# Scatter DMAs of the expert gates in groups of four behind waits for ScalarE, and the low parts of 24 weight units made by VectorE instead of GpSimd

## The chip, the cores and the metric

One core of one Trainium2 chip runs the whole program. The time is device microseconds of one execution; the times below are those of several executions and their median, and a profile is one further execution under the profiler.

## What is computed

Two transformer blocks over 512 tokens of width 1024, in fp32. The change lies in the expert layer (PEER) of the first block:

```python
q = (ht @ wq).reshape(T, PEER_HEADS, 2, PEER_HALF)
sc = jnp.einsum('thpd,hpnd->thpn', q, subkeys)
v1, i1 = lax.top_k(sc[:, :, 0], PEER_TOPK)          # 8 heads, 16 best of 128 keys, twice
v2, i2 = lax.top_k(sc[:, :, 1], PEER_TOPK)
cand = (v1[..., :, None] + v2[..., None, :]).reshape(T, PEER_HEADS, PEER_TOPK * PEER_TOPK)
best, pos = lax.top_k(cand, PEER_TOPK)
experts = e1 * PEER_KEYS + e2                        # 128 experts of 16384 for each token
gates = jax.nn.softmax(best, axis=-1)
act = jax.nn.gelu(jnp.einsum('tkd,td->tk', u_tab[experts], x))
out = jnp.einsum('tk,tkd->td', gates * act, v_tab[experts])
```

Before it stand sliding-window attention and a pooling mixer, after it the second block: differential attention, a short convolution and two gated feed-forward layers.

## The kernel before

**Units.** All weights are 486 units of 128 x 1024 fp32 (512 KB). A unit is loaded by the queue of SP into a ring of eight buffers (`RING`), ScalarE rounds it to its high part (`split_hi`, L1062), and the low part, raw minus high, is made in the place of the raw data by GpSimd (`low_part`, L509, four quarters of 256 columns) or by VectorE (`unit_low`, L1765, in one instruction). A product with it is three matmuls (`mm3`, L593 to L595): high by high, low by high, high by low. TensorE starts a unit when its low part is there (`unit_in`) and signals `unit_used` at its end; ScalarE makes the high part of unit u + 5 after that of unit u (`AHEAD`), and SP loads unit u + 8.

**The stage of the expert scores** multiplies all 16384 rows of `u_tab` (key units 0 to 127, 24 matmuls of 512 columns each) with the 512 tokens; after each unit ScalarE applies the gelu (L1264) and every four units stores 1024 KB to `act_dram`. Beside it VectorE, in one fixed order of instructions, selects the experts of the token tiles 1, 2, 3, 0 (`select`), and for tiles 1 to 3 sums the gates of equal experts (`join_gates`: seven steps of growing size, 128x512 to 128x2048, on `same` and `gate_sums`) and gives them free for scattering (`gates_made`). Low parts of key units from 28 on (`LOW_FROM`) are placed between these steps by `lows(n)`. From unit 56 on VectorE makes one low part per unit and two products of the modulation sums of the second block (`ada_part`, L1781 and L1783; two instructions a tile for the first 16 tiles, one for the other 80), whose 96 tiles of 512 KB SP loads from unit 51 on, two a unit; TensorE adds a short sum after every fourth unit (`ada_sum`). This is the ada stage below, units 56 to 103.

**The scatters.** GpSimd writes the gates of tiles 1 to 3 into a dense table `gate_dram` (128 units x 128 rows x 384 tokens) with 384 indirect DMAs of 128 elements (`scatter`, L547), 16 to a token tile and head, in the order of `SCATTERS`; a tile's next head waits until the one before has landed. Before the change GpSimd also makes the low parts of 24 key units (`BESIDE`: 30, 34, 38, 42, 47, ... 127), a quarter after each four scatters; before the first quarter it waits for the unit's high part. So the scatters are held to the pace of the units. After unit 124 (`LOADS_AT`) ScalarE waits for all scatters and loads the first gates and activations.

**The stage of the expert values** multiplies gates and activations (`gp`, 384 tokens) with `v_tab`, 128 value units; the 128 tokens of tile 0 are done by gathering rows instead (L533, L541, L1945).

The lines that count in what follows: L509 GpSimd's quarter, L547 the scatter, L593 to L595 the matmuls of a unit, L1062 a high part, L1264 the gelu, L1274 and L1280 the loads of gates and activations, L1765 VectorE's low part, L1781 and L1783 the ada products. Unit numbers are those of key units unless value units are named.

Of the kernel before, what the change touches and what calls it, by code (L numbers as in the profile page):

```python
# [16 lines left out]
F32 = mybir.dt.float32  # L17
# [4 lines left out]
ALU = mybir.AluOpType  # L22
AX_X = mybir.AxisListType.X

P = 128
D = 1024
# [16 lines left out]
TOPK = 16  # L43
# [10 lines left out]
U_PEER = U_WQ + 2 * PEER_HEADS  # L54
# [3 lines left out]
U_DIFF = U_PEER + 2 * P  # L58
# [8 lines left out]
RING = 8  # L67
# [8 lines left out]
LOW_FROM = 28  # L76
ORDER = (1, 2, 3, 0)
EXP_AT = (5, 17, 29, 45)
SCATTERS = [(1, 0), (2, 0), (1, 1), (2, 1)] + [s for h in range(6) for s in ((3, h), (1, h + 2), (2, h + 2))] \
    + [(3, 6), (3, 7)]  # L80
BESIDE = [30 + 17 * n // 4 for n in range(len(SCATTERS))]
ZEROS = 8
LOADS_AT = P - 4
BUNCH = 4
SPAN = 8
ROWS = 4
# [1 line left out]
LAG = AHEAD - 1  # L88
# [30 lines left out]
def build_program(nc, w_units, x_in, ctx_in, params, consts, consts2, trig, pool_w, subkeys, ada_w, out,  # L119
                  rel_dram, gate_dram, act_dram, x_dram):  # L120
    KB = 1024
    with ExitStack() as ctx:
# [16 lines left out]
        hi = at("unit_hi", 0, [P, RING, D], F32R)  # L139
        lo = at("unit_lo", 32 * KB, [P, RING, D], F32R)  # L140
        raw = at("unit_raw", 32 * KB, [P, RING, D])
# [166 lines left out]
        hi_ready, lo_ready, unit_used = sem("hi_ready"), sem("lo_ready"), sem("unit_used")  # L308
        value_lo_ready = sem("value_lo_ready")
# [194 lines left out]

        @block.gpsimd
        def _(pool):
            def quarter(u, part):
                cols = slice(part * (D // 4), (part + 1) * (D // 4))
                return nc.gpsimd.tensor_tensor(lo[:, u % RING, cols], raw[:, u % RING, cols],  # L509
                                               hi[:, u % RING, cols].bitcast(F32), ALU.subtract)  # L510

            def low_part(u, per=0, i=None):

                pool.wait_ge(hi_ready, u + 1 if i is None else i * per + (u + 1))
                for part in range(4):
                    last = quarter(u, part)
                last.then_inc(lo_ready, 1)

            def low_range(a, b):
                while a < b and a % RING:  # L520
                    low_part(a)
                    a += 1
                n = max(0, (b - a) // RING)
                if n:
                    with pool.Fori(0, n) as i:
                        for k in range(RING):
                            low_part(a + k, RING, i)
                for u in range(a + n * RING, b):
                    low_part(u)

            def pick(k):

                pool.indirect_dma_start(picked[:, k:k + 1], None, act_dram.rearrange("u j (t o) -> (u j t) o", o=1),  # L533
                                        bass.IndirectOffsetOnAxis(act_at[:, k:k + 1], 0))\
                    .then_inc(picks_in[k // PICKS], 16)

            def fetch(k):

                if k >= ROWS:
                    pool.wait_ge(row_added, k - ROWS + 1)  # L540
                pool.indirect_dma_start(vrows[:, k % ROWS, :], None, w_units.rearrange("u p n -> (u p) n"),  # L541
                                        bass.IndirectOffsetOnAxis(row_at[:, k:k + 1], 0))\
                    .then_inc(rows_in[k % ROWS], 16)

            def scatter(t, k):

                pool.indirect_dma_start(gate_dram.rearrange("i j (t o) -> (i j t) o", o=1),  # L547
                                        bass.IndirectOffsetOnAxis(gidx[:, t - 1, k:k + 1], 0),
                                        gsum[:, t - 1, k:k + 1], None).then_inc(scattered[t - 1], 16)

            nc.gpsimd.memset(zero[:, :], 0.0).then_inc(zero_made, 1)
            low_range(0, U_PEER + LOW_FROM)
            pool.wait_ge(zeroed, 16 * ZEROS)
            for n, (t, h) in enumerate(SCATTERS):
                if h == 0:
                    pool.wait_ge(gates_made, t)
                else:
                    pool.wait_ge(scattered[t - 1], 16 * TOPK * h)
                for k in range(TOPK):
                    scatter(t, TOPK * h + k)  # L560
                    if k % 4 == 3:
                        if k == 3:
                            pool.wait_ge(hi_ready, U_PEER + BESIDE[n] + 1)
                        last = quarter(U_PEER + BESIDE[n], k // 4)
                last.then_inc(lo_ready, 1)
            pool.wait_ge(mine_at, 2)
            pool.wait_ge(unit_used, U_VALUES)
            for s in a_stored:
                pool.wait_ge(s, 16 * (P // BUNCH // 2))
            for k in range(PICKS):  # L570
                pick(k)
            for k in range(ROWS):
                fetch(k)
            for k in range(ROWS, G):
                ahead = PICKS + 2 * (k - ROWS) if k < ROWS + PICKS else 2 * PICKS - ROWS + k
                for n in range(ahead, ahead + (2 if k < ROWS + PICKS else 1)):
                    if n < G:
                        pick(n)
                fetch(k)
            low_range(U_DIFF + LAG, N_UNITS)  # L580
# [3 lines left out]
        def _(pe):  # L584
# [11 lines left out]

            def unit_in(u, per=0, i=None):
                made, n = lo_ready, u + 1
                before = sum(U_PEER + b < u for b in BESIDE)
                if u - U_PEER in BESIDE:  # L600
                    n = U_PEER + LOW_FROM + before + 1
                elif U_PEER + LOW_FROM <= u < U_DIFF + LAG:
                    made, n = value_lo_ready, u + 1 - (U_PEER + LOW_FROM) - before
                elif u >= U_DIFF + LAG:
                    n -= U_DIFF + LAG - (U_PEER + LOW_FROM) - before
                pe.wait_ge(made, n if i is None else i * per + n)

            def project(u, dst, ah, al, per=0, i=None, ready=None):
# [95 lines left out]
            for n in range(10):  # L704
                u = U_WIN + n
# [4 lines left out]
                else:  # L710
                    band_scores(0)
                    unit_in(u)
                    for t in range(TT):
                        tok = slice(t * P, (t + 1) * P)
                        for c in range(DC):
                            wh, wl = unit_chunk(u, c)
                            last = mm3(ps[:, n % 4, tok], hn_hi[:, c, tok], hn_lo[:, c, tok], wh, wl,
                                       c == 0, c == DC - 1)
# [11 lines left out]
            for t in range(TT):  # L730
# [5 lines left out]
                for s in range(2 * HEADS):  # L736
                    last = nc.tensor.transpose(PTp[:, s, :], E[t][:, s // 2, (s % 2) * P:(s % 2 + 1) * P], ident)
# [776 lines left out]
        def _(dve):  # L1514
# [247 lines left out]
            def unit_low(u):  # L1762

                dve.wait_ge(hi_ready, u + 1)
                V.tensor_tensor(lo[:, u % RING], raw[:, u % RING], hi[:, u % RING].bitcast(F32),  # L1765
                                ALU.subtract).then_inc(value_lo_ready, 1)
# [33 lines left out]
            def lows(n):  # L1800

                for u in range(key_lows[0], min(key_lows[0] + n, P + LAG)):
                    if u not in BESIDE:
                        unit_low(U_PEER + u)
                key_lows[0] += n

            def select(t, between):
# [80 lines left out]
            select(1, 0)  # L1888
            join_gates(1, (0,) * 7)
            select(2, 0)  # L1890
            join_gates(2, (0, 0, 0, 0, 0, 0, 1))
            select(3, 2)
            join_gates(3, (1, 1, 2, 1, 1, 2, 1))
            select(0, 2)
# [272 lines left out]
            for j in range(DC):  # L2167
                b = j % 2
# [176 lines left out]
```

## Time and profile before

| | |
|---|---|
| runs | 3044.7, 3061.32, 3061.61 us, median 3061.32 |
| profiled execution | 3072.2 us, of which the span of the trace is 3070.4 |
| TensorE busy | 2875.8 us, 94% |
| VectorE, ScalarE, GpSimd busy | 1762.4 us (57%), 983.9 us (32%), 1704.7 us (56%) |
| mean granted clock of TensorE | 0.968 |

Busy times of engines overlap, and those of TensorE's instructions are modelled, so a busy engine is not one at its peak. A granted clock of 1.00 is 2.4 GHz, one of 0.50 is 1.2 GHz. Key units 28 to 127 lie between 442 and 1116 us of the span and the value units from 1120 on.

### The profile page before, as it was taken

What the parts mean: (1) busy time and instruction counts of PE and PEld (TensorE: products, weight loads), DVE (VectorE), ACT (ScalarE), POOL (GpSimd) and SP (SyncE); (2) the same over time, 40 slices, a digit from 0 to 9 for tenths busy, and PEclk for the clock granted to TensorE, in tenths of its full rate; (3) what the DMA queues carried; (4) which work ended last, traced back from release to release, by engine and by line L of the source; (5) the groups of instructions that cost most, each with busy time, mean ns of one, the idle gap of its engine ahead of it and who ended that gap; (6) DMA issues with size and microseconds to landing.
All of it is one profiled execution on the core that took longest, in us unless ns stands there. A gap on an engine that the chain in (4) does not pass through costs nothing.

```text
span 3070.4 us, 39204 instructions
## 1 busy us (share of the span) xinstructions
PE 2875.8 (94%) x14484; PEld 2443.1 (80%) x14484; DVE 1762.4 (57%) x2726; ACT 983.9 (32%) x1472; POOL 1704.7 (56%) x1757
## 2 busy tenths in 40 slices
PE   8799988888989988999999989999999989999999
PEld 6698877677777778999999858558888868898887
DVE  6568997665553136778887773674333353343333
ACT  4432322222222333333333433783322222232211
POOL 5144877788888755688753123002554545555553
PEclk9899999999999999999999999999999999999999
DMA  6932443378875467999997211101323323233332
GB/s 202 342 97 83 153 129 98 122 250 284 289 267 186 124 209 283 325 338 347 355 350 276 90 55 50 38 1 59 97 90 102 96 76 96 72 108 103 97 95 75
DMA packets 191662, 499.40 MB, mean 163 GB/s; under 512 B 29608, under 2 KB 80936, under 8 KB 190888
## 3 DMA queue, kind: packets, MB, share of 16 engines
q1 hardware_dynamic: 104528, 338.95, 33.4%
q10 hardware_dynamic: 52184, 91.23, 8.4%
q0 software_dynamic: 34816, 67.41, 6.3%
q8 instruction: 86, 1.41, 0.2%
q14 instruction: 48, 0.39, 0.0%
HBM read 432.82 MB, written 64.68 MB: 162 GB/s over the span
## 4 chain that ended last, share of the span: by engine, by line
PE 57%; POOL 21%; DVE 11%; issue 6%; ACT 3%; DMA 2%; another core or an unknown queue 0%; SPq 0%; ACTq 0%; DVEq 0%
PE ps L593 17%; PE ps L595 17%; PE ps L594 17%; POOL gate_dram L547 13%; POOL value_rows L541 3%; POOL picked L533 3%; POOL unit_lo L509 3%; PE ps L917 2%; DVE nb L2000 1%; PE ps L937 1%; DMA unit_raw<-w_units 1%; DVE same L1858 1%; DVE same L1856 1%; DVE gate_sums L1860 1%; PE ps L928 1%
## 5 line engine op out<-in xcount | busy, mean ns | idle before, releaser
L509 POOL TENSOR_TENSOR unit_lo<-unit_raw,unit_hi 128x256 fp32r<-128x256 f32 x1112 | 876.5, 820 | 1049.3 <-ACT unit_hi L1062 1046.5
L593 PE MATMUL ps<-hn_hi,unit_hi 128*128 128x512 f32 (+1 forms) x2344 | 922.8, 394 | 107.3 <-POOL unit_lo L509 74.1
L594 PE MATMUL ps<-hn_lo,unit_hi 128*128 128x512 f32 (+1 forms) x2344 | 904.6, 386 | 0.0
L595 PE MATMUL ps<-hn_hi,unit_lo 128*128 128x512 f32 (+1 forms) x2344 | 903.9, 386 | 0.0
L1062 ACT ACTIVATE unit_hi<-unit_raw 128x1024 fp32r<-128x1024 f32 x486 | 505.7, 1055 | 487.2 <-DMA unit_raw<-w_units 372.8
L593 PEld LDWEIGHTS ps<-hn_hi,unit_hi 128*128 128x128 f32 x2344 | 449.2, 192 | 218.6 <-issue 103.0
L594 PEld LDWEIGHTS ps<-hn_lo,unit_hi 128*128 128x128 f32 x2344 | 449.5, 192 | 88.9 <-issue 4.9
L547 POOL DMA_INDIRECT gate_dram<-gate_sums,gate_at x384 | 460.6, 1199 | 104.1 <-issue 103.4
L595 PEld LDWEIGHTS ps<-hn_hi,unit_lo 128*128 128x128 f32 x2344 | 448.3, 191 | 87.8
L1765 DVE TENSOR_TENSOR unit_lo<-unit_raw,unit_hi 128x1024 fp32r<-128x1024 f32 x208 | 259.8, 1250 | 185.9 <-ACT unit_hi L1062 150.1
L593 PE MATMUL ps<-gp_hi,unit_hi 128*128 128x384 f32 x1024 | 349.2, 341 | 18.2 <-DVE gp_lo L1927 14.2
L595 PE MATMUL ps<-gp_hi,unit_lo 128*128 128x384 f32 x1024 | 346.8, 339 | 3.9 <-issue 3.9
L594 PE MATMUL ps<-gp_lo,unit_hi 128*128 128x384 f32 x1024 | 346.9, 339 | 3.1 <-issue 3.0
L1264 ACT ACTIVATE stage<-ps 128x512 f32<-128x512 f32 x128 | 76.5, 598 | 610.1 <-PE ps L595 570.8
L541 POOL DMA_INDIRECT value_rows<-w_units,row_at x128 | 191.1, 1493 | 123.5 <-DVE own_values L1945 79.8
L2128 DVE TENSOR_TENSOR pf<-gel,ps 128x512 f32<-128x512 f32 x44 | 30.3, 688 | 380.8 <-PE ps L595 380.8
L593 PEld LDWEIGHTS ps<-gp_hi,unit_hi 128*128 128x128 f32 x1024 | 195.6, 191 | 24.0 <-DVE gp_lo L1927 13.8
L533 POOL DMA_INDIRECT picked<-act_dram,act_at x128 | 176.0, 1375 | 62.4 <-issue 38.7
L595 PEld LDWEIGHTS ps<-gp_hi,unit_lo 128*128 128x128 f32 x1024 | 195.6, 191 | 4.8 <-issue 4.8
L594 PEld LDWEIGHTS ps<-gp_lo,unit_hi 128*128 128x128 f32 x1024 | 195.8, 191 | 4.6 <-issue 4.6
L1945 DVE SCALAR_TENSOR_TENSOR own_values<-value_rows,picked,own_values 128x1024 f32<-128x1024 f32 x127 | 162.8, 1282 | 51.3 <-DMA value_rows<-w_units,row_at 40.3
L1481 ACT ACTIVATE gel<-ps 128x512 f32<-128x512 f32 x44 | 26.4, 599 | 495.4 <-PE ps L595 495.4
(280 smaller groups left out, 3862.4 us busy)
## 6 DMA issues: line engine op xcount, KB each, us to landing
unit_raw<-w_units SPq DMA_DIRECT2D x486, 512.0 KB
araw<-ada_units SPq DMA_DIRECT2D x96, 512.0 KB
act_dram<-stage ACTq DMA_DIRECT2D x32, 1024.0 KB
gate_dram<-zero SPq DMA_DIRECT2D x8, 3072.0 KB, 23.6
gbuf<-gate_dram ACTq DMA_DIRECT2D x16, 1536.0 KB
abuf<-act_dram ACTq DMA_DIRECT2D x32, 768.0 KB
gate_dram<-gate_sums,gate_at POOLq DMA_INDIRECT x384
x<-x_t SPq DMA_DIRECT2D x8, 256.0 KB, 6.1
```

The lines of the kernel that those rows point to most:

```text
L509: return nc.gpsimd.tensor_tensor(lo[:, u % RING, cols], raw[:, u % RING, cols], hi[:, u % RING, cols].bitcast(F32), ALU.subtract)
L533: pool.indirect_dma_start(picked[:, k:k + 1], None, act_dram.rearrange("u j (t o) -> (u j t) o", o=1), bass.IndirectOffsetOnAxis(act_at[:, ...
L541: pool.indirect_dma_start(vrows[:, k % ROWS, :], None, w_units.rearrange("u p n -> (u p) n"), bass.IndirectOffsetOnAxis(row_at[:, k:k + 1] ...
L547: pool.indirect_dma_start(gate_dram.rearrange("i j (t o) -> (i j t) o", o=1), bass.IndirectOffsetOnAxis(gidx[:, t - 1, k:k + 1], 0), gsum[ ...
L593: mm(dst, wh, ah, start=start, stop=False)
L594: mm(dst, wh, al, start=False, stop=False)
L595: return mm(dst, wl, ah, start=False, stop=stop)
L917: last = mm(SD[m][:, keys], Qd[rows, 4 * m + h // 2, qt * P:(qt + 1) * P], Kd[rows, 4 * m + h // 2, keys], start=True, stop=True)
L1062: activation(hi[:, u % RING], raw[:, u % RING], ACT.Copy).then_inc(hi_ready, 1)
L1264: activation(stage[:, g % 2, u % BUNCH], ps[:, u % 4, :], ACT.Gelu).then_inc(gel_done, 1)
L1765: V.tensor_tensor(lo[:, u % RING], raw[:, u % RING], hi[:, u % RING].bitcast(F32), ALU.subtract).then_inc(value_lo_ready, 1)
L1945: last = V.scalar_tensor_tensor(own[:, :], vrows[:, k % ROWS, :], picked[:, k:k + 1], own[:, :], ALU.mult, ALU.add)
```

## The change

Four things change in the key stage:

- The quarters go out of the scatters: GpSimd makes no low part of key units 28 to 127, and `BESIDE` and all that counts with it go.
- Each four scatters (`BURST`) wait for ScalarE: group b of the 96 waits for the high part of key unit 29 + 102 b // 96 (`STEPS`). The first waits for unit 29's, the last for unit 129's.
- VectorE makes the low parts of all key units from 28 on, 24 more than before, in `lows`. Since `lows` doesn't leave units out any more, units move to other places too. In the second join, one stands before the last step and two behind it, where one stood behind it.
- ScalarE waits for the scatters after unit 126 instead of 124.

```diff
-BESIDE = [30 + 17 * n // 4 for n in range(len(SCATTERS))]
-LOADS_AT = P - 4
+LOADS_AT = P - 2
+BURST = 4
+STEPS = 102
...
                 for k in range(TOPK):
+                    burst, of = (TOPK * n + k) // BURST, TOPK * len(SCATTERS) // BURST
+                    if k % BURST == 0:
+                        pool.wait_ge(hi_ready, U_PEER + LOW_FROM + STEPS * burst // of + 2)
                     scatter(t, TOPK * h + k)
-                    if k % 4 == 3:
-                        if k == 3:
-                            pool.wait_ge(hi_ready, U_PEER + BESIDE[n] + 1)
-                        last = quarter(U_PEER + BESIDE[n], k // 4)
-                last.then_inc(lo_ready, 1)
...
             def lows(n):

                 for u in range(key_lows[0], min(key_lows[0] + n, P + LAG)):
-                    if u not in BESIDE:
-                        unit_low(U_PEER + u)
+                    unit_low(U_PEER + u)
                 key_lows[0] += n
...
             select(2, 0)
-            join_gates(2, (0, 0, 0, 0, 0, 0, 1))
+            join_gates(2, (0, 0, 0, 0, 0, 1, 2))
             select(3, 2)
```

`low_part` takes in the code of `quarter`, and `unit_in` on TensorE waits for VectorE's counter for every key unit from 28 on.

## Rows read from the trace of the kernel before

**Rows 1.** The page's busy times: us (share of the span) x instructions

```profile
PE 2875.8 (94%) x14484; PEld 2443.1 (80%) x14484; DVE 1762.4 (57%) x2726; ACT 983.9 (32%) x1472; POOL 1704.7 (56%) x1757
```

**Rows 2.** Waits of TensorE, 280 to 1300 us: us in total, times, longest

```profile
PE ps L593 <- POOL unit_lo L509: 74.1, 21, 8.4
PE ps L593 <- DVE unit_lo L1765: 10.5, 2, 5.7
```

**Rows 3.** Table by stretches: length, then each engine's busy us (instructions), clock, DMA

```profile
core 0: us, PE busy (x) PEld busy (x) DVE busy (x) ACT busy (x) POOL busy (x), PEclk, DMA share, GB/s
...
468.60:546.80 78.20, 68.05 (x286) 55.10 (x284) 60.79 (x49) 21.75 (x29) 66.01 (x52) 0.93 0.40 122
...
680.00:960.00 280.00, 251.20 (x1113) 199.28 (x1112) 150.75 (x134) 65.31 (x85) 230.38 (x201) 0.95 0.80 270
...
1120.00:1620.00 500.00, 479.24 (x2665) 471.73 (x2665) 378.61 (x469) 168.72 (x232) 345.76 (x244) 0.97 0.91 328
```

**Rows 4.** Line of time, ScalarE's gelus after units 26, 27, 28, 79, 80, 102

```profile
436.61 0.60 ACT L1264 ACTIVATE stage<-ps 128x512 f32<-128x512 f32 x1 [3.89 <-PE ps L595]
...
442.05 0.60 ACT L1264 ACTIVATE stage<-ps 128x512 f32<-128x512 f32 x1 [3.89 <-PE ps L595]
...
454.53 0.60 ACT L1264 ACTIVATE stage<-ps 128x512 f32<-128x512 f32 x1 [10.94 <-PE ps L595]
...
800.97 0.60 ACT L1264 ACTIVATE stage<-ps 128x512 f32<-128x512 f32 x1 [3.89 <-PE ps L595]
...
807.21 0.60 ACT L1264 ACTIVATE stage<-ps 128x512 f32<-128x512 f32 x1 [4.69 <-PE ps L595]
...
959.61 0.60 ACT L1264 ACTIVATE stage<-ps 128x512 f32<-128x512 f32 x1 [10.99 <-PE ps L595]
```

**Rows 5.** Line of time, GpSimd, the four quarters of unit 123

```profile
1062.38 0.75 POOL L509 TENSOR_TENSOR unit_lo<-unit_raw,unit_hi 128x256 fp32r<-128x256 f32 x1
1063.30 0.99 POOL L547 DMA_INDIRECT gate_dram<-gate_sums,gate_at  x1 [0.16 <-issue]
...
1077.93 1.95 POOL L547 DMA_INDIRECT gate_dram<-gate_sums,gate_at  x1 [0.30 <-issue]
...
1081.16 0.75 POOL L509 TENSOR_TENSOR unit_lo<-unit_raw,unit_hi 128x256 fp32r<-128x256 f32 x1
```

**Rows 6.** Line of time, VectorE: units 28, 29, 31 and 32, ada products, unit 126

```profile
445.47 1.23 DVE L1765 TENSOR_TENSOR unit_lo<-unit_raw,unit_hi 128x1024 fp32r<-128x1024 f32 x1
...
458.81 1.22 DVE L1765 TENSOR_TENSOR unit_lo<-unit_raw,unit_hi 128x1024 fp32r<-128x1024 f32 x1
...
466.28 2.36 DVE L1765 TENSOR_TENSOR unit_lo<-unit_raw,unit_hi 128x1024 fp32r<-128x1024 f32 x2
...
640.17 10.51 DVE L1783 SCALAR_TENSOR_TENSOR ada_sums<-araw,csilu,ada_sums 128x1024 f32<-128x1024 f32 x8
...
1077.83 1.23 DVE L1765 TENSOR_TENSOR unit_lo<-unit_raw,unit_hi 128x1024 fp32r<-128x1024 f32 x1 [4.21 <-issue]
```

**Rows 7.** Table by stretches of the scatters alone (L547): length, busy (instructions)

```profile
450.00:600.00 150.00, 98.39 (x79) 0.92 0.36 109
...
680.00:960.00 280.00, 191.00 (x161) 0.95 0.80 270
960.00:1107.00 147.00, 98.53 (x90) 0.97 0.45 140
```

**Rows 8.** The same of VectorE's low parts alone (L1765)

```profile
680.00:960.00 280.00, 42.84 (x32) 0.95 0.80 270
```

**Rows 9.** The same of the ada products alone (L1783)

```profile
680.00:960.00 280.00, 95.08 (x70) 0.95 0.80 270
```

**Rows 10.** Line of time, all engines, from the last scatter to the value stage

```profile
1105.45 0.95 POOL L547 DMA_INDIRECT gate_dram<-gate_sums,gate_at  x1 [0.30 <-issue]
...
1108.38 0.39 ACTq L1274 DMA_DIRECT2D gbuf<-gate_dram  x1
...
1115.34 0.39 PE L595 MATMUL ps<-hn_hi,unit_lo 128*128 128x512 f32 x1
...
1119.79 0.51 PE L593 MATMUL ps<-gp_hi,unit_hi 128*128 128x384 f32 x1 [4.07 <-DVE gp_lo L1927]
```

More of the change, by code:

```diff
@@ L506, in _ @@
         def _(pool):
[L507 to L510, printed above, removed]
             def low_part(u, per=0, i=None):
@@ L515, in low_part @@
                 for part in range(4):
-                    last = quarter(u, part)
+                    cols = slice(part * (D // 4), (part + 1) * (D // 4))
+                    last = nc.gpsimd.tensor_tensor(lo[:, u % RING, cols], raw[:, u % RING, cols],
+                                                   hi[:, u % RING, cols].bitcast(F32), ALU.subtract)
                 last.then_inc(lo_ready, 1)
@@ L598, in unit_in @@
                 made, n = lo_ready, u + 1
[L599 to L603, printed above, removed]
+                if U_PEER + LOW_FROM <= u < U_DIFF + LAG:
+                    made, n = value_lo_ready, u + 1 - (U_PEER + LOW_FROM)
                 elif u >= U_DIFF + LAG:
-                    n -= U_DIFF + LAG - (U_PEER + LOW_FROM) - before
+                    n -= U_DIFF + LAG - (U_PEER + LOW_FROM)
                 pe.wait_ge(made, n if i is None else i * per + n)
```

## The prediction

> **What bounds the kernel now.** Of the page I read the busy times first [rows 1]: TensorE has 94% of the span, so the question is where its other 6%, and its half-speed stretches, lie. The waits of TensorE answer that for the stretch of the expert scores [rows 2]: 21 waits, 74.1 us together, for the low parts that GpSimd makes (L509), and two, 10.5 us, for those of VectorE (L1765). The table of stretches [rows 3] shows what follows a wait: the mean granted clock is 0.93 from 468.6 to 546.8 us and 0.95 from 680 to 960, so part of that time went by at the lower of the clock's two levels (1.2 GHz) instead of the upper (2.4). ScalarE's gelus show the step [rows 4]: a key unit ends every 5.44 us when nothing is late (436.61 to 442.05); unit 28 took 12.48 us (442.05 to 454.53) with a wait of some 4.8 us in it, so a wait of 5 costs 7.
>
> From 442.05 (unit 27 done) to 1115.7 (unit 127 done, [rows 10]) are 673.7 us for 100 units. Unhindered they are 544 us, and some 11 us for the twelve sums of the ada stage (a unit with one in it is 6.24 us, 800.97 to 807.21 in [rows 4]) and one context sum on TensorE: 555. So **119 us** are to be had here at most.
>
> GpSimd's own line of time shows why it is late [rows 5]. Its first quarter of unit 123 starts at 1062.38, the last ends at 1081.91: twelve indirect DMAs lie between, each 0.96 us or more and 0.30 of issue behind it, about 20 us, while TensorE wants the unit 21 us after its high part. The loop has no slack, hence the 21 waits for its 24 units. At the end everything meets: the last DMA ends at 1106.4, ScalarE starts the loads of gates at 1108.38, and the first product of the value stage is at 1119.79 [rows 10], 13.4 us after the last scatter.
>
> **The change, part by part.** *Quarters off GpSimd.* 96 instructions and their waits go; with them the 74.1 us of waits and the slow clock behind them. What can be late next: VectorE's low parts, the scatters as such, and the data.
>
> *Low parts on VectorE.* 24 more at 1.2 us (windows of L1765: 42.84 us for 32 in [rows 8], with the disturbed ones 1.34), 29 to 32 us in all. VectorE was busy 150.75 of 280 us from 680 to 960 [rows 3], so they are hidden where they come in time, and cost TensorE 1.2 us each, some 30 in all, where they don't. I follow it from the second join by [rows 6]; that a unit is wanted every 5.44 us is [rows 4]. Unit 28's low part now stands before the last step of that join: it ends at 439.7 instead of 446.7, before TensorE wants it at 442.05, and that stall of 7 us goes. The last step (7 us) is over at 446.7; units 29 and 30 follow, to 449.1, where unit 29 is wanted at 447.5: 0.4 us late. Then the third selection. From the end of unit 28's low part to the start of the next were 12.2 us (446.6 to 458.8), so units 31 and 32 are made from 461.2: 31 is ready at 462.4 and wanted at 458.8. This is a stall of 3.7 us, 5 to 6 with the slow clock (as 4.8 was 7): one of the two first stalls stays, moved. Unit 31 is done at 469.8. The next group comes 6.3 us later (units 33, 34, ready 472), wanted at 480. From there to the end of the third join VectorE has 60.8 us of its own work (the stretch 468.6 to 546.8 in [rows 3]) and three low parts more, so with 1 us of gaps the third join ends at 472.2 + 61.9 + 3.6 = **538 us** (before: 546.8), and no high part holds it up: the last one that it needs, of unit 47, is there after unit 42 is done, at 530 + 1.6. TensorE runs from 469.8 at 5.44: unit 34 done at 486, unit 55 at 600, all low parts of the stretch being ready 5 us or more ahead.
>
> *Ada stage.* For the first 16 ada tiles VectorE has two products a tile: eight of them took 10.51 us [rows 6], so a unit costs 5.3 + 1.2 = 6.5 us against TensorE's 5.6. It is ahead by some 8 us and loses 0.9 a unit over eight units: just enough, a stall of 0 to 5 us. After that two ada products (95.08 us for 70 in [rows 9], 1.36 each, 1.2 of it to the next one's start) and a low part are 3.9 us a unit. Data: 3 x 0.524 MB and 0.262 MB of stores are 1.84 MB a unit; the stretch moved 270 GB/s at a share of 0.80 [rows 3], so 338 at full share, 5.4 us a unit against 5.6. No loss, but no room either. TensorE would end unit 127 at 486 + 93 x 5.44 + 10 = **1002 us**, 1003 to 1010 with those.
>
> *Scatters with pauses.* 96 groups of four wait for high parts, one group every 102/96 = 1.06 units, 5.8 us (6.0 in the ada stage); the last waits for unit 129's, 987 us. The wait as an instruction costs at most the 0.17 that a quarter's neighbours had as issue [rows 5], 16 us if 96 of them add it; it lies in front of a scatter's own 0.30, so I take nothing. Nothing is queued behind a pause but scatters, and only ScalarE's loads of gates wait for those. So the question is GpSimd's own rate. Per scatter with its 0.30 of issue: 98.39/79 + 0.30 = 1.55 us (450 to 600), 191.00/161 + 0.30 = 1.49 (680 to 960), 98.53/90 + 0.30 = 1.39 (960 to 1107) [rows 7]. A scatter on a quiet VectorE takes 1.26 [rows 5]; the excess belongs to VectorE's instructions that run at that moment. In 680 to 960 the excess was 161 x 0.23 = 36 us over 102 low parts and ada products, 0.36 us each, 0.42 if GpSimd had been in scatters all of the time. Now there are three per unit in 5.64 us, so 4.4 us are left for scatters of 1.26: 3.5 a unit, **1.62 us each**. In the late stretch 12 us over 26 such instructions, 0.47 to 0.8 each: 1.39 to 1.47, I take 1.43.
> The third token tile's gates come at 538; by then GpSimd has done its first 64 scatters (some 99 us from 427) and stands idle. 320 are left: 34 to 590 us (1.55), 167 over the 48 ada units to 861 (1.62), 119 at 1.43 to **1031 us**. That is 40 us behind the pauses' schedule, so from 538 on hardly a pause is waited for: they cost nothing and do nothing. Bounds for the end: 1.26 a scatter lets the schedule rule, 992; the highest mean seen in a long stretch (1.55) gives 538 + 496 = 1034, and twice the excess of 680 to 960 (1.26 + 0.46 = 1.72) gives 1088. I take 1031, near the rows of the ada stage itself.
>
> *The trace against a rule.* A scatter that meets a low part of VectorE is longer here: 1.95 us at 1077.93 [rows 5], with L1765 running from 1077.83 to 1079.06 [rows 6], against 0.96 to 0.99 of its quiet neighbours. The Trainium skill, "SBUF — State Buffer", section "Who interferes with whom", says that a VectorE instruction with two SBUF inputs contends with GpSimd's reads alone, and that descriptor generation needs the write interface, an inference, so that `tensor_tensor` would not stall a DMA. By that rule the first rival below would hold. The trace disagrees at the rows just named.
>
> *ScalarE's place for the loads* moves from unit 124 to 126. As it waits for the last scatter in both kernels, this costs nothing; from the last scatter to the value stage stay 13.4 us [rows 10], since gates must be read (1108.38) before the first product. If the scatters are early, it costs: the loads start 1.6 us after unit 126 ends, the value stage 11.4 us after that (1108.38 to 1119.79), 7 us of idle TensorE.
>
> **Sum.** Value stage at 1031 + 13.4 = 1045 instead of 1119.8: 75 us less. What follows is tied to that point and to the data (328 GB/s, share 0.91, [rows 3]) and doesn't change. The profiled execution had 3070.4 us of span and 3072.2 in all, so 2997; against the median of the runs, 3061.3, it is **2986 us**.
>
> **Rivals.** *The schedule rules* (scatters at 1.26 to 1.45): TensorE ends unit 126 at 997, value stage at 997 + 1.6 + 11.4 = 1010, 110 us less: 2951. For it: fewer collisions, as no quarter of GpSimd's disturbs VectorE (its low parts took 1.22 us when alone and 1.34 in the mean of [rows 8]). Against: three VectorE instructions a unit. *VectorE or the data lag in the ada stage*: TensorE keeps there the 6.93 us a unit that units 81 to 102 had (807.21 to 959.61 in [rows 4]) instead of 5.64: 48 x 1.29 = 62 us, unit 127 at 1064, value stage 8 us later at 1072: 48 us less, 3013. For it: 0.9 us a unit lost over eight units, and a share of DMA near 1; against: the stage has only to catch up with the scatters, so its first 25 us are free. *The waits only change their name*: VectorE's low parts come in bunches between other steps and TensorE stalls as often as now, a third of the 119 is won: 3022. Against: where the lows now stand, only the two waits of [rows 2] are for L1765. *Slower*: the scatters meet so many VectorE instructions that each takes the 1.95 us of the disturbed one in [rows 5] and 0.30, 2.25 together: 538 + 720 = 1258, 152 us later than now, and 3213 us in all, with TensorE idle in front of the value stage. It decides at (1106 - 538)/320 = 1.78 us a scatter.
>
> **Chances.** Forecast 0.55; schedule 0.22; lag in the ada stage 0.12; new names 0.06; slower 0.05. The range takes the first three in and their bounds: 2945 to 3020. A measurement of this kernel tells 1% from no change. Faster by over 1% are the first three and most of the fourth, 0.93; within 1% 0.03; slower 0.04.
>
> **What the changed profile would show.** No wait of TensorE for L509 between 442 and 1107; granted clock near 1.00 from 470 to 1000; one wait of some 4 us for L1765 near 459; unit 127 done at 1003 to 1010; scatters back to back from 538 at a mean of 1.2 to 1.35 us, the last at about 1030; ScalarE at the loads of gates waiting for it some 30 us, and TensorE as long. If the last scatter ends near 992, the first rival is right; if the gelus are over 6 us apart from unit 60 on, the second. Wrong from the ground would be waits of TensorE for low parts again, or scatters over 1.78 us.

## The result, and the profile after

The changed kernel took 2952.84 us in the median of four runs (2942.5 to 2964.3) beside 3056.2 of the kernel before (3044.7 to 3061.6): ratio 0.967, 95% interval 0.962 to 0.972. Two further groups of runs gave 0.970 (0.966 to 0.974) and 0.972 (0.968 to 0.975). Single executions of one kernel lie up to 37 us apart (13 of the kernel before: 3029.6 to 3066.7), so medians of four say little about 5 us. In the changed kernel lines are a few numbers lower: L589 to L591 are the matmuls, L545 is the scatter, L1758 VectorE's low part, L1776 its ada product, L1055 the high part, L1257 the gelu, L1267 and L1273 the loads of gates and activations.

The waits of TensorE, 280 to 1300 us of the profiled execution (2964.3 us, span 2962.5), beside [rows 2]:

```profile
PE ps L589 <- DVE gp_lo L1919: 28.8, 4, 20.8
PE ps L589 <- DVE unit_lo L1758: 3.5, 2, 3.3
```

The 21 waits for GpSimd are gone, of the 10.5 us for VectorE's low parts 3.5 are left, and the wait before the first product of the value stage grew from 4.1 us [rows 10] to 20.8. The table by stretches, beside [rows 3] (the columns are the same; the ada stage is 600 to 861 here):

```profile
468.60:546.80 78.20, 78.20 (x344) 64.62 (x343) 75.43 (x92) 24.69 (x32) 59.83 (x42) 0.99 0.49 148
600.00:861.00 261.00, 261.00 (x1214) 209.47 (x1213) 186.73 (x175) 71.17 (x92) 207.68 (x176) 1.00 0.94 323
...
861.00:1005.00 144.00, 144.00 (x642) 118.63 (x641) 36.96 (x42) 45.69 (x63) 109.00 (x105) 1.00 0.48 147
```

TensorE has no gap from 600 to 1005 and the upper clock throughout. What took the place of the waits stands at the end of the key units, in the line of time of all engines, beside [rows 10]:

```profile
1000.66 1.05 ACT L1055 ACTIVATE unit_hi<-unit_raw 128x1024 fp32r<-128x1024 f32 x1
...
1005.18 0.39 PE L591 MATMUL ps<-hn_hi,unit_lo 128*128 128x512 f32 x1
...
1012.95 0.96 POOL L545 DMA_INDIRECT gate_dram<-gate_sums,gate_at  x1 [0.30 <-issue]
1015.31 0.39 ACTq L1267 DMA_DIRECT2D gbuf<-gate_dram  x1
...
1026.38 0.66 PE L589 MATMUL ps<-gp_hi,unit_hi 128*128 128x384 f32 x1 [20.81 <-DVE gp_lo L1919]
```

ScalarE is done with unit 126's work at 1001.7 and stands until the last scatter has landed; its loads start at 1015.3 and TensorE, done at 1005.6, at 1026.4. Before, that point was 1119.8: 93 us. GpSimd's waits from 400 to 1030 us show how little the pauses did:

```profile
POOL gate_dram L545 <- issue: 115.5, 379, 0.3
POOL gate_dram L545 <- ACT unit_hi L1055: 13.7, 4, 7.0
...
POOL gate_dram L545 <- DMA gate_dram<-gate_sums,gate_at: 3.6, 1, 3.6
```

Of the four waits for ScalarE two are the usual 0.30 us of issue, so of 96 pauses two were waited for, 7.0 and 6.2 us; the second ends at 474.5. Scatters then ran back to back to 1013.9 but for 3.6 us before the last head, whose predecessor had not landed.

Of the 107.9 us between the two spans 93 are there at the start of the value stage, 13 more arise in that stage (573 us before, 560 after) and under 2 behind it. In the first profile of before, eight single matmuls between 1152 and 1163 us were held up by up to 2 us each (8.1 us, "issue" in the waits: nothing that the profile shows). That is not all of it: a second profile of before shows no such thing, and its value stage took 568 us. In twelve profiles of other kernels it took 542 to 563, three of them of the same changed kernel (560, 556, 542). Medians of the three groups put the changed kernel 103, 96 and 93 us under the kernel before.

### The profile page after: what moved, and what is told of

The parts are those of the page before. It is cut to its first block, busy times and chain, and to the rows that moved or that the text cites. A ratio compares the mean times of both kernels' runs of the same rounds, so it can differ in the third digit from the quotient of the medians.

```text
span 2962.5 us, 39158 instructions
## 1 busy us (share of the span) xinstructions
PE 2837.0 (96%) x14484; PEld 2422.6 (82%) x14484; DVE 1771.3 (60%) x2750; ACT 985.7 (33%) x1472; POOL 1619.2 (55%) x1661
## 4 chain that ended last, share of the span: by engine, by line
PE 59%; POOL 19%; DVE 11%; issue 6%; ACT 2%; DMA 2%; SPq 0%; ACTq 0%; POOLq 0%; DVEq 0%
PE ps L589 18%; PE ps L591 17%; PE ps L590 17%; POOL gate_dram L545 12%; POOL picked L531 4%; POOL value_rows L539 3%; PE ps L910 2%; DVE nb L1992 1%; PE ps L930 1%; DMA unit_raw<-w_units 1%; DVE same L1850 1%; DVE same L1848 1%; DVE gate_sums L1852 1%; DMA value_rows<-w_units,row_at 1%; PE ps L921 1%
## 5 line engine op out<-in xcount | busy, mean ns | idle before, releaser
L513 POOL TENSOR_TENSOR unit_lo<-unit_raw,unit_hi 128x256 fp32r<-128x256 f32 x1016 | 785.0, 810 | 1019.5 <-ACT unit_hi L1055 1018.9
L589 PE MATMUL ps<-hn_hi,unit_hi 128*128 128x512 f32 (+1 forms) x2344 | 910.9, 389 | 25.7 <-DVE hn_lo L1625 10.4
L590 PE MATMUL ps<-hn_lo,unit_hi 128*128 128x512 f32 (+1 forms) x2344 | 895.6, 382 | 0.0
L591 PE MATMUL ps<-hn_hi,unit_lo 128*128 128x512 f32 (+1 forms) x2344 | 895.5, 382 | 0.0
L1055 ACT ACTIVATE unit_hi<-unit_raw 128x1024 fp32r<-128x1024 f32 x486 | 505.7, 1055 | 466.5 <-DMA unit_raw<-w_units 359.4
L589 PEld LDWEIGHTS ps<-hn_hi,unit_hi 128*128 128x128 f32 x2344 | 443.2, 189 | 127.8 <-issue 19.4
L545 POOL DMA_INDIRECT gate_dram<-gate_sums,gate_at x384 | 458.1, 1193 | 132.8 <-issue 115.5
L590 PEld LDWEIGHTS ps<-hn_lo,unit_hi 128*128 128x128 f32 x2344 | 443.4, 189 | 87.6 <-issue 4.9
L591 PEld LDWEIGHTS ps<-hn_hi,unit_lo 128*128 128x128 f32 x2344 | 443.0, 189 | 85.3
L589 PE MATMUL ps<-gp_hi,unit_hi 128*128 128x384 f32 x1024 | 347.1, 339 | 36.7 <-DVE gp_lo L1919 36.5
L1758 DVE TENSOR_TENSOR unit_lo<-unit_raw,unit_hi 128x1024 fp32r<-128x1024 f32 x232 | 282.3, 1220 | 113.0 <-ACT unit_hi L1055 112.1
L591 PE MATMUL ps<-gp_hi,unit_lo 128*128 128x384 f32 x1024 | 345.1, 337 | 0.0
L1257 ACT ACTIVATE stage<-ps 128x512 f32<-128x512 f32 x128 | 76.6, 598 | 492.3 <-PE ps L591 473.1
L589 PEld LDWEIGHTS ps<-gp_hi,unit_hi 128*128 128x128 f32 x1024 | 194.7, 190 | 41.0 <-issue 21.2
L531 POOL DMA_INDIRECT picked<-act_dram,act_at x128 | 187.0, 1461 | 58.9 <-issue 38.7
L1937 DVE SCALAR_TENSOR_TENSOR own_values<-value_rows,picked,own_values 128x1024 f32<-128x1024 f32 x127 | 162.7, 1281 | 61.4 <-DMA value_rows<-w_units,row_at 57.4
L591 PEld LDWEIGHTS ps<-gp_hi,unit_lo 128*128 128x128 f32 x1024 | 194.3, 190 | 0.0
## 6 DMA issues: line engine op xcount, KB each, us to landing
gbuf<-gate_dram ACTq DMA_DIRECT2D x16, 1536.0 KB, 19.5
```

What stands on the lines that cost most here:

```text
L513: last = nc.gpsimd.tensor_tensor(lo[:, u % RING, cols], raw[:, u % RING, cols], hi[:, u % RING, cols].bitcast(F32), ALU.subtract)
L589: mm(dst, wh, ah, start=start, stop=False)
L590: mm(dst, wh, al, start=False, stop=False)
L591: return mm(dst, wl, ah, start=False, stop=stop)
L1055: activation(hi[:, u % RING], raw[:, u % RING], ACT.Copy).then_inc(hi_ready, 1)
L1257: activation(stage[:, g % 2, u % BUNCH], ps[:, u % 4, :], ACT.Gelu).then_inc(gel_done, 1)
```

## The experiments

All times of points are of each run's own profiled execution, us from its start; the start of the key stage alone moves by up to 4 us between executions of one kernel.

| run | us (median) | ratio to before | last scatter ends | wait of TensorE | value stage starts |
|---|---|---|---|---|---|
| before | 3056 | | 1106.4 | 4.1 | 1119.8 |
| before, again | 3066.8 (one) | | 1103.4 | 8.3 | 1118 |
| changed | 2952.8 | 0.967 | 1013.9 | 20.8 | 1026.4 |
| changed, again | 2961.0 | 0.970 | 1009.8 | 22.1 | 1022.4 |
| changed, third | 2952.7 | 0.972 | 1010.7 | 19.5 | 1023.1 |
| dummy quarters | 3047.1 | 0.998 | 1101.5 | 113.9 | 1114.1 |
| quarters together | 3034.7 | 0.993 | 1085.7 | 19.5 | 1098.7 |
| half the scatters | 2947.1 | 0.966 | 996.6 | 8.4 | 1016.4 |
| no pauses | 2959.8 | 0.968 | 1007.7 | 18.1 | 1021.2 |
| loads at 124 | 2958.3 | 0.970 | 1010.0 | 20.9 | 1022.9 |
| one low in the join | 2966.3 | 0.971 | 1011.6 | 14.1 | 1027.5 |
| one-input ada | 2945.4 | 0.968 | 997.9 | 8.2 | 1013.3 |
| early scatters, 126 | 2945.1 | 0.971 | 1000.6 | 13.4 | 1018.7 |
| early scatters, 124 | 2949.6 | 0.970 | 1000.4 | 14.2 | 1017.2 |

Theory A: what counts is the time of GpSimd, whose last scatter sets the start of the value stage, before the change as after it. Its main rival D: TensorE's waits for the spread quarters, and the slow clock after them, were the cost.

**The changed kernel, twice more.** 

> The changed kernel once more, as the measure for the other runs of this group. Theory A (GpSimd's rate of scatters sets the start of the value stage): about 2953 us, last scatter at about 1014 us of the span, a wait of TensorE of about 21 us before the value stage. A rival, that these 21 us are an accident of one execution, expects a wait under 5 us.

> The changed kernel once more, the measure for the runs of this group: 2950 to 2962 us, last scatter at 1008 to 1014, value stage from 1022 to 1027.

The wait before the value stage was 22.1 and 19.5 us: no accident. The first of the two took 2961.0 us, 8 more than expected.

**Dummy quarters.** GpSimd keeps a quarter's work, and nobody waits for it.

```diff
+        dummy = at("dummy", R1 + 28 * KB + 512, [P, D // 2])
...
+            pool.wait_ge(consts_in, 16)
...
                     scatter(t, TOPK * h + k)
+                    if k % 4 == 3:
+                        made = (TOPK * n + k) // 4
+                        if made:
+                            pool.wait_ge(sem('dummy_made'), made)
+                        nc.gpsimd.tensor_tensor(dummy[:, 0:D // 4], con[:, 0:D // 4], con[:, D // 4:D // 2],
+                                                ALU.subtract)\
+                            .then_inc(sem('dummy_made'), 1)
```

> After each four scatters GpSimd subtracts 128x256 values as before the change, but from constants into a place that nobody reads. No low part hangs on it. Theory A (the quarters cost as time of GpSimd): low parts stay in time and TensorE ends the last key unit at 1005 as in the changed kernel, but the last scatter comes 96 x 0.9 to 1.0 = 86 to 96 us later, at 1100 to 1110, and TensorE waits some 105 us there; 3035 to 3050 us, nearly all of the gain lost. Rival D (the quarters cost because TensorE waited for them, 21 times, and for its clock after that): at most 15 us slower than the changed kernel, 2953 to 2968.

Measured: ratio 0.998 (0.996 to 1.001), the gain is gone. TensorE's waits from 430 to 1130 us, and GpSimd's groups of 420 to 1110 us (busy us, mean ns, idle before them):

```profile
PE ps L598 <- DVE gp_lo L1928: 113.9, 1, 113.9
PE ps L598 <- DVE unit_lo L1767: 3.3, 1, 3.3
```

```profile
L546 POOL DMA_INDIRECT gate_dram<-gate_sums,gate_at x384 | 474.1, 1235 | 111.7 <-issue 101.5 <-ACT unit_hi L1064 8.9 <-DMA gate_dram<-gate_sums,gate_at 0.7
L568 POOL TENSOR_TENSOR dummy<-con 128x256 f32<-128x256 f32 x96 | 93.8, 977 | 2.2
```

No key unit waits for GpSimd, and the time is that of before all the same, as one wait of 114 us in place of 21 small ones. 93.8 us of quarters moved the last scatter by 87.6 us. This rules D out: without the waits for quarters the time is not better while GpSimd has the work. It does not say that the waits were free. In the kernel before both bounds lay together, TensorE done at 1115.7 and the loads of gates begun at 1108.4 [rows 10]; the quarters on GpSimd stand behind both, and no run has the waits without the work.

**Quarters together.** The kernel before, with each of GpSimd's low parts made in one piece and the same work.

```diff
-                    if k % 4 == 3:
-                        if k == 3:
-                            pool.wait_ge(hi_ready, U_PEER + BESIDE[n] + 1)
-                        last = quarter(U_PEER + BESIDE[n], k // 4)
-                last.then_inc(lo_ready, 1)
+                    if k == 3:
+                        pool.wait_ge(hi_ready, U_PEER + BESIDE[n] + 1)
+                        for part in range(4):
+                            last = quarter(U_PEER + BESIDE[n], part)
+                        last.then_inc(lo_ready, 1)
```

> The kernel before, but with the four quarters of a unit one behind the other right after the wait for its high part instead of spread over sixteen scatters; as much work on GpSimd as before. Theory A (work of GpSimd counts): the waits of TensorE for low parts of GpSimd nearly go (74 us before), but the last scatter stays at 1090 to 1106, where the time goes into the wait before the value stage; at most 15 us faster than before, 3040 to 3056 us. Rival D (the spread quarters made TensorE late, and that alone cost): 2960 to 2990 us.

Measured: ratio 0.993 (0.991 to 0.996), 21 us faster; 6 more than A allowed, far from D. TensorE still waited 46.1 us in 15 waits for those low parts, where A had said that they nearly go, and 19.5 before the value stage. GpSimd itself waited only 10.5 us for high parts in the whole stretch, so it mostly came late to them:

```profile
PE ps L593 <- POOL unit_lo L509: 46.1, 15, 6.9
PE ps L593 <- DVE gp_lo L1927: 19.5, 1, 19.5
```

The last scatter came 20.7 us earlier, and GpSimd's own groups account for it: the scatters took 439.6 us instead of 460.6 and its waits for high parts 10.5 instead of 28.3, while the quarters took 7 us more, the issues 10 and waits for a landed head 2. Why scatters are shorter when quarters stand together was not tried.

**Half the scatters.** This leaves out every second scatter, and with it half of the gates.

```diff
-                    pool.wait_ge(scattered[t - 1], 16 * TOPK * h)
+                    pool.wait_ge(scattered[t - 1], 8 * TOPK * h)
...
-                    scatter(t, TOPK * h + k)
+                    if k % 2 == 0:
+                        scatter(t, TOPK * h + k)
...
-                        act.wait_ge(s, 16 * SLOTS)
+                        act.wait_ge(s, 8 * SLOTS)
```

> Of each token tile and head only 8 of the 16 scatters are issued, so half of the gates are left out. Theory A: the schedule of the pauses rules now, the last scatter is at about 990, ScalarE doesn't wait at unit 126, and TensorE stands 5 to 9 us before the value stage, the time that gates and activations need to land: value stage at 1007 to 1011 instead of 1022 to 1026, 2938 to 2946 us. Rival C (what the stage starts earlier it gives back by its data): 2950 or more.

Measured: now the pauses rule (GpSimd's waits, 430 to 1000 us):

```profile
POOL gate_dram L545 <- ACT unit_hi L1056: 256.3, 83, 15.3
```

The last scatter ended at 996.6, before ScalarE was at its loads (1002.9), and 8.4 us of TensorE's wait stay while they land. The time is 2947.1, 6 to 14 us under the three medians of the changed kernel, though the intervals overlap (0.966, 0.961 to 0.971): about what the late scatters still cost. The value stage started at 1016.4, not at 1007 to 1011 as A had it, and the time lies between A's 2946 and C's 2950.

**No pauses.**

```diff
-                    burst, of = (TOPK * n + k) // BURST, TOPK * len(SCATTERS) // BURST
-                    if k % BURST == 0:
-                        pool.wait_ge(hi_ready, U_PEER + LOW_FROM + STEPS * burst // of + 2)
                     scatter(t, TOPK * h + k)
```

> No scatter waits for ScalarE. Theory A: the pauses were waited for only at the start (13.7 us in four waits before 475 us), so the scatters start at 423 instead of 430, the third tile's gates hold them up a little at 538, and the last scatter ends 7 to 13 us earlier, at 1001 to 1007; the value stage starts as much earlier; 2940 to 2948 us. Rival B (the pauses spare the data queues or TensorE's low parts): without them new waits of TensorE before 1000 us, 2955 us or more. Rival C (what the value stage starts earlier it gives back, as it is bound by its data): the last scatter moves, the time doesn't, 2950 to 2956.

The last scatter came 2 to 6 us earlier, not 7 to 13: 5.9 us were spent in waiting for a tile's gates instead. The time, 2959.8 (0.968, 0.963 to 0.972), is that of the changed kernel beside it, 2961.0, and above what A (2940 to 2948) and C (2950 to 2956) expected. No new wait of TensorE appeared, so B falls; C can't be told from A by so little.

**Loads at 124.** `LOADS_AT = P - 4` again.

> ScalarE waits for the scatters after unit 124 again. The last scatter decides in both, so the loads of gates start at the same time, 1015. Theory A: the high parts of units 130 and 131 come later but before they are wanted, 2953 to 2957 us. Rival E (ScalarE's lead at the start of the value stage counts): the low parts of value units 2 and 3 are late, 3 to 8 us slower.

Same points, same time. The change of this number does nothing while the scatters are late.

**One low in the join.**

```diff
-            join_gates(2, (0, 0, 0, 0, 0, 1, 2))
+            join_gates(2, (0, 0, 0, 0, 0, 0, 1))
```

> The changed kernel with one low part behind the last step of the second join, as before, and none before it. Unit 28 is late again by some 5 us and two more stalls of 3 to 6 us follow behind it, since the following groups hold the same number of units and start one unit earlier: TensorE ends the key units 10 to 20 us later, at 1012 to 1022. Theory A: the last scatter at 1010 to 1014 still decides, so the value stage starts at most 8 us later and the time is 2953 to 2966. A rival, that these stalls count in full, expects 2966 to 2978.

TensorE waited 10.1 us for low parts instead of 3.5 and ended the key units 8 to 13 us later (at 1013.3; 1005.6, 1000.3 and 1003.7 in the changed kernel), and the wait before the value stage shrank from 20 to 22 us to 14.1. In the value stage's start 1 to 5 us are left of it. The median, 2966.3, stands on the border of the two expectations, and the ratio (0.971, 0.966 to 0.976) decides nothing; the points of the profile do. Three low parts in the second join in place of one are worth little here: they let TensorE arrive earlier at a wait.

**One-input ada.** It leaves out the summing of the modulation of the second block.

```diff
-                        last = V.scalar_tensor_tensor(part, araw[m % ADA_SLOTS][:, :], c, part, ALU.mult, ALU.add)
+                        last = V.tensor_scalar(part, araw[m % ADA_SLOTS][:, :], c, None, ALU.mult)
```

> The modulation sums of the second block are left out: each ada product is a tensor_scalar with one input from SBUF and doesn't add to the sum before it. Theory F (VectorE's instructions with two SBUF inputs lengthen the scatters): scatters in the ada stage fall from a mean of about 1.22 us to 1.05 to 1.10, the last one is at 987 to 995, held by the pauses, and the value stage starts at 1006 to 1011; 2938 to 2946 us. Rival G (the length comes from the DMA queues or the data traffic of that stage): the mean stays over 1.17 and the last scatter over 1004; 2950 to 2960.

The table of scatters alone from 590 to 861 us, first of the changed kernel, then of this one:

```profile
590.00:861.00 271.00, 215.85 (x182) 1.00 0.94 324
```

```profile
590.00:861.00 271.00, 212.46 (x193) 1.00 0.93 324
```

1.186 us a scatter became 1.101 with the same data traffic (324 GB/s), so G, the traffic, is ruled out. The last scatter came at 997.9 and the value stage at 1013.3, 3 and 2 us after the expected; the time (0.968, 0.964 to 0.971) isn't distinct from that of the changed kernel beside it (0.972).

F named the second input, but the instructions also became shorter (74.19 us for 98, 0.76 each, against 1.27), and the traces show that it is their length that fell and not the effect of one. This is a scatter of this run that began in a one-input product, GpSimd's row first:

```profile
730.03 1.47 POOL L545 DMA_INDIRECT gate_dram<-gate_sums,gate_at  x1 [0.30 <-issue]
```

```profile
729.92 0.75 DVE L1776 TENSOR_SCALAR ada_sums<-araw,csilu 128x1024 f32<-128x1024 f32 x1 [0.43 <-DMA araw<-ada_units]
```

It takes 1.47 us instead of 0.96 and ends 0.83 us after the product. Scatters beside two-input instructions end 0.82 to 0.84 us after them too (rows below). So F is right in that VectorE's instructions lengthen the scatters, and wrong in that only those with two inputs do.

**Early scatters.** No pauses; eight scatters between GpSimd's last low parts; another order of heads; loads at 126 or 124.

```diff
+SCATTERS = [(1, 0), (2, 0), (1, 1), (2, 1), (1, 2), (3, 0), (2, 2), (1, 3), (3, 1), (2, 3), (1, 4), (3, 2),
+            (2, 4), (1, 5), (3, 3), (2, 5), (1, 6), (3, 4), (2, 6), (3, 5), (1, 7), (3, 6), (2, 7), (3, 7)]
...
+            for u in range(6 * RING, U_PEER + LOW_FROM):
+                low_part(u)
+                k = u - (U_PEER + LOW_FROM - EARLY)
+                if k >= 0:
+                    if k == 0:
+                        pool.wait_ge(zeroed, 16 * ZEROS)
+                        pool.wait_ge(gates_made, 1)
+                    scatter(1, k)
```

> No pauses; the first eight scatters stand between GpSimd's last low parts, one after each of units 20 to 27; the third tile's heads come later in the order and never two in a row before the last. Theory A: the waits of the run without pauses for the gates (5.9 us) and for a landed head (3.7 us) go, and eight scatters use idle time of GpSimd: last scatter at 985 to 993, before ScalarE is past unit 126, whose loads then start at about 998; value stage at 1007 to 1010 instead of 1022 to 1026; 2938 to 2947 us. A rival, that the early scatters make GpSimd's low parts late, expects waits of TensorE for them before 440 us.

> The same with ScalarE's loads of gates after unit 124. Theory A: loads start at 987 to 993, gates and activations land before TensorE ends the key units at about 1001, and its wait shrinks to under 5 us: value stage at 1002 to 1006, 2932 to 2942 us, 15 to 20 under the changed kernel. Rival C (given back in the value stage by its data): value stage as early, but 2946 or more.

The last scatter came 10 us earlier than in the changed kernel of the same group, half of what was expected; 4.7 us went into a wait for the second tile's gates. TensorE waited for no low part of GpSimd. The value stage started only 4 to 6 us earlier, and TensorE's wait with the loads at 124, expected under 5 us, was 14.2. From the first load of gates to the first product were 14.8 and 15.4 us in these two runs, against 11.1 in the changed kernel (1015.31 to 1026.38). In these two SP's queue moved 1.57 MB beside the loads, the last weight unit and the context, which in the changed kernel went before them; whether that is the reason was not tried. The times (0.971, 0.967 to 0.975, and 0.970, 0.967 to 0.973) are not distinct from those of the changed kernel beside them (0.972, 0.968 to 0.975). No version is shown to beat it.

**The kernel before, again.** 

> The kernel before once more, for a second profile. Theory A: last scatter at 1100 to 1108 us, value stage from 1114 to 1121. In the first profile the value stage took 573 us, with single matmuls held up by up to 2 us each between 1152 and 1163, against 555 to 562 in all profiles of changed kernels. If that was an accident, the stage takes 555 to 563 here; rival C (a stage that starts without a wait has its data late) expects 570 or more again.

Last scatter 1103.4, 72.0 us in 21 waits for GpSimd, value stage 568 us: between the two expectations, and over that of every kernel but the first profile of before. C is not borne out by the other profiles: the stage took 555 us after a wait of 8.4 (half the scatters) and 555 after one of 113.9 (dummy quarters). The traces show where the difference between profiles lies, though: TensorE's waits in the stage, behind its first product, were 21 us in both profiles of before, 17 to 20 in the three that took 563 us, 3.3 in the one that took 542. Why both profiles of before are at the upper end stays open.

## Why the prediction was right, and where it was not

The range held the time and the sign was right; the forecast, 2986, was 33 us too slow.

- *The quarters are GpSimd's time; without them its scatters are the next bound*: shown by the dummy quarters. TensorE ended its last key unit at 1005.6 (1003 to 1010 predicted).
- *The second join*: units 28 and 29 ready at 441.0 and 449.2, one stall of 3.3 us moved to unit 31, the third join done at 538.1 (538 predicted). These rows are VectorE's line of time after the change, beside [rows 6]:

```profile
439.81 1.22 DVE L1758 TENSOR_TENSOR unit_lo<-unit_raw,unit_hi 128x1024 fp32r<-128x1024 f32 x1
...
447.92 2.44 DVE L1758 TENSOR_TENSOR unit_lo<-unit_raw,unit_hi 128x1024 fp32r<-128x1024 f32 x2
...
462.47 2.36 DVE L1758 TENSOR_TENSOR unit_lo<-unit_raw,unit_hi 128x1024 fp32r<-128x1024 f32 x2
...
537.91 0.23 DVE L1855 TENSOR_SCALAR gate_at<-sel 128x128 int32<-128x128 f32 x1
```

ScalarE's gelus after units 27 and 34 give the price of the stall:

```profile
443.80 0.60 ACT L1257 ACTIVATE stage<-ps 128x512 f32<-128x512 f32 x1 [3.89 <-PE ps L591]
...
488.68 0.60 ACT L1257 ACTIVATE stage<-ps 128x512 f32<-128x512 f32 x1 [3.89 <-PE ps L591]
```

The seven units took 44.9 us instead of 38.1, so 6.8 were lost, near the 5 to 6 for the stall and the 0.4 at unit 29 that were counted. More than the wait of 3.3 us is lost because TensorE ran at the lower clock behind it (0.52 granted from 464 to 470).

- *The ada stage has no room, but suffices*: no wait of TensorE in it; 323 GB/s at a share of 0.94.
- *Pauses cost nothing and do nothing from 538 on*: right, by the waits and by the run without them.
- *Scatters at 1.62 us in the ada stage and 1.43 late*: **the term that was mis-sized.** They took 215.85/182 + 0.30 = 1.49 (590 to 861) and 115.77/112 + 0.30 = 1.33 (861 to 1014), from these rows of the changed kernel:

```profile
545.00:590.00 45.00, 36.46 (x29) 1.00 0.50 161
590.00:861.00 271.00, 215.85 (x182) 1.00 0.94 324
861.00:1014.00 153.00, 115.77 (x112) 0.98 0.48 148
```

The last scatter was therefore at 1014 instead of 1031. I had charged 0.42 us of excess to each of VectorE's two-input instructions, the 0.36 of before raised for a GpSimd that never pauses. Measured from 600 to 861: 176 scatters x 0.22 = 39 us over 48 low parts and 93 ada products, 0.27 each. So the mean scatter of the ada stage stayed at the 1.19 us of before [rows 7], though VectorE had more to do beside it. The lines of time say how (GpSimd's first, then VectorE's):

```profile
479.90 0.96 POOL L545 DMA_INDIRECT gate_dram<-gate_sums,gate_at  x1 [0.30 <-issue]
...
656.34 1.32 POOL L545 DMA_INDIRECT gate_dram<-gate_sums,gate_at  x1 [0.31 <-issue]
...
747.64 1.83 POOL L545 DMA_INDIRECT gate_dram<-gate_sums,gate_at  x1 [0.30 <-issue]
749.77 1.52 POOL L545 DMA_INDIRECT gate_dram<-gate_sums,gate_at  x1 [0.30 <-issue]
...
756.35 2.03 POOL L545 DMA_INDIRECT gate_dram<-gate_sums,gate_at  x1 [0.30 <-issue]
758.69 1.08 POOL L545 DMA_INDIRECT gate_dram<-gate_sums,gate_at  x1 [0.30 <-issue]
```

```profile
478.79 2.29 DVE L1833 TENSOR_REDUCE sel<-dec 128x128 f32<-128x2048 f32 x1
...
656.07 0.75 DVE L1774 TENSOR_SCALAR ada_sums<-araw,csilu 128x1024 f32<-128x1024 f32 x1 [3.54 <-DMA araw<-ada_units]
...
747.35 1.28 DVE L1776 SCALAR_TENSOR_TENSOR ada_sums<-araw,csilu,ada_sums 128x1024 f32<-128x1024 f32 x1 [1.42 <-DMA araw<-ada_units]
...
749.24 1.21 DVE L1758 TENSOR_TENSOR unit_lo<-unit_raw,unit_hi 128x1024 fp32r<-128x1024 f32 x1
...
756.27 2.67 DVE L1776 SCALAR_TENSOR_TENSOR ada_sums<-araw,csilu,ada_sums 128x1024 f32<-128x1024 f32 x2
```

A scatter that starts within a TENSOR_TENSOR, a SCALAR_TENSOR_TENSOR or a TENSOR_SCALAR of 128x1024 ends 0.83 us after it (749.24 + 1.21 = 750.45; 749.77 + 1.52 = 751.29), whatever its number of inputs; one within a TENSOR_REDUCE keeps its 0.96 us (479.90). Counted over the fourteen traces, for scatters that began at least 0.12 us after the instruction and 0.2 before its end: held so were all 1571 in the first two kinds, 87 of 89 in the third and none of 158 in a TENSOR_REDUCE. So one instruction holds at most one scatter. Of a pair of them (756.27) the first holds one scatter for 1.07 us; the next scatter can't start before 0.30 us behind that, near the end of the second instruction, and loses 0.12. Counted for all such 128x1024 instructions of the stretch, one that stood directly behind another cost 0.20 us, one that did not 0.30; from 680 to 960 before, these were 0.20 and 0.36. Of 111 before 25 stood behind another, of 152 after 66. That is why the charge did not grow with density as I had it; the fall from 0.36 to 0.30 stays unexplained, and the pairs were not varied in a run.

In the late stretch I divided 12 us by 26 instructions; the table of before has 18 low parts from 960 to 1107, so the charge was 0.67 each and not 0.47. The changed kernel has 26 from 861 to 1014, at 0.35 each.

- *The first 64 scatters, 99 us from 427*: 115 us from 430. A pause held them 6.2 us at 474.5, and each took 1.70 us with its issue, not 1.55, as the joins and the selection beside them hold many TENSOR_TENSORs of up to 2.3 us. GpSimd never stood idle for the third tile's gates. The last 320 took 469 us instead of 493: 7 us too few up to the first of these, 24 too many behind it.
- *The rest*: value stage at 1026.4 against 1045 makes 19 of the 33 us. The other 14 lie behind that point, which I had taken as unchanged: 13 in the value stage and under 2 after it. The sum was made against a profile whose value stage is the longest of fourteen, and why the kernel before has long ones stays open. In the medians a part of it shows too: the sum started from 3061.3, that of three runs, and that of four is 3056.2.
- The first rival gave 2951, next to the measured time, and was not what happened: the schedule never ruled, and ScalarE waited for the scatters. Its value stage was at 1010, 16 us too early, and it had the same 14 us too many behind it, so its number was met by luck. The Trainium skill ("SBUF — State Buffer", "Who interferes with whom") says that a probe found no `tensor_tensor`, with both inputs in SBUF, that stalls a DMA, and infers as the reason that the making of descriptors on GpSimd needs the write interface. The 1.52 us above, beside a TENSOR_TENSOR, and the 1.95 of [rows 5] speak against it for these indirect DMAs.

## What to carry to other kernels

When an engine delivers many small things late, ask whether it is late by order or by its sum of work: keep its work and cut the dependence, as the dummy quarters do, and one run tells. A bound that shows as 21 waits can come back as a single one of 114 us with the same time of the kernel. Removing stalls of an engine ahead of a common gate is worth nothing until what the gate waits for is faster (three low parts in the join in place of one: at most 5 us).

## What was not expected of the hardware

The same kernel's value stage took 542, 556 and 560 us in three executions. The waits show it: behind its first product TensorE waited 3.3, 12.8 and 15.7 us in it for VectorE's `gp_lo`, and VectorE, which works in a fixed order, waited 23, 51 and 57 us there for the gathered rows of tile 0 (`own_values`, L1937). Why the rows came later was not tried; a change of 5 to 10 us ahead of this stage is not seen in four runs.

And a scatter's length follows VectorE's instruction of the moment, though it moves only 128 elements: 0.96 us beside a reduction, and until 0.83 us after the end of a TENSOR_TENSOR, a SCALAR_TENSOR_TENSOR or a TENSOR_SCALAR of 128x1024 that runs when it starts, with one input or two. A short instruction in its place, and not one with fewer inputs, made the scatters faster.
